# Loading each expert chunk as two half transfers, released and awaited half by half

## The reference, cut to what matters

```python
h = rmsnorm(x, ln_mix);  proj = h @ w_in              # pooling heads and gated DeltaNet heads
x = x + concat([pool_out, dn_out]) @ w_out
h = rmsnorm(x, ln_moe)
top_vals, top_idx = top_k(h @ router_w + router_b, 4) # 4 of 32 experts per token
gates = softmax(top_vals)
for each block of rows of one expert e:
    gt  = minimum(xblk @ w_gate[e] + b_gate[e], 7)
    up  = clip(xblk @ w_up[e] + b_up[e], -7, 7)
    hid = (up + 1) * (gt * sigmoid(1.702 * gt))
    y   = hid @ w_down[e] + b_down[e]                 # added to its tokens times their gates
x = x + y
x = x + (p @ w_ple) * sigmoid(rmsnorm(x, ln_ple) @ w_ple_gate)
return rmsnorm(x, final_norm), and the new pool, conv and delta-rule states
```

## Time and profile before

| | |
|---|---|
| median of the runs | 1196.0 us |
| the profiled execution | 1194.54 us |
| its span, first to last instruction | 1192.8 us |
| PE busy | 1130.2 us, 95% |
| moved by DMA | 435.16 MB, mean 365 GB/s |
| issues of whole expert chunks | 62 gate, 62 up, 57 down in the ring, one gate beside it |

### The profile page before, as it was taken

The page is one execution under the profiler, slowest core; times in us unless marked ns, Lnnn a source line. Parts: engine busy times, 40 slices in busy tenths (PEclk is TensorE's granted clock), DMA queues, the critical chain, the costliest instruction groups (busy, mean ns, idle before and its releaser), DMA issues.

```text
span 1192.8 us, 15407 instructions
## 1 busy us (share of the span) xinstructions
PE 1130.2 (95%) x5906; PEld 485.3 (41%) x5936; DVE 411.5 (34%) x781; ACT 213.7 (18%) x398; POOL 40.0 (3%) x118
## 2 busy tenths in 40 slices
PE   8999999999999999999999898999999999899997
PEld 5667865433333332333333333333333333233333
DVE  5756765843132222132223231323131313131325
ACT  3444232321101021011010101011101101010025
POOL 6002110000000000000000000000000000000000
PEclk9999999999999999999999999999999999999999
DMA  9821539789999999999999999999999999999941
GB/s 315 251 105 71 166 117 333 296 337 424 427 426 428 427 428 428 427 427 429 428 427 429 428 425 428 429 428 427 429 430 428 427 429 429 428 427 427 419 163 45
DMA packets 50603, 435.16 MB, mean 365 GB/s; under 512 B 6861, under 2 KB 14554, under 8 KB 24812
## 3 DMA queue, kind: packets, MB, share of 16 engines
q1 hardware_dynamic: 44425, 430.22, 87.3%
q10 hardware_dynamic: 6123, 4.18, 1.1%
HBM read 429.54 MB, written 4.11 MB: 364 GB/s over the span
## 4 chain that ended last, share of the span: by engine, by line
PE 69%; DMA 21%; DVE 6%; issue 2%; ACT 2%; SPq 0%; POOL 0%; DVEq 0%; ACTq 0%; POOLq 0%
PE ps L1782 40%; DMA ring<-in_w_gate 18%; PE ps L1309 7%; PE ps L1728 4%; PE ps L1619 3%; PE ps L1224 2%; DMA ring<-in_w_up 2%; PE ps L1508 2%; PE ps L1356 1%; PE ps L1749 1%; DVE x_resid L2500 1%; PE ps L1423 1%; PE ps L1996 1%; PE ps L1973 1%; PE ps L1854 1%
## 5 line engine op out<-in xcount | busy, mean ns | idle before, releaser
L1782 PE MATMUL ps<-ring,ht_region 128*64 128x512 f32 (+1 forms) x2152 | 453.7, 599 | 18.9 <-DMA ring<-in_w_gate 18.6
L1782 PEld LDWEIGHTS ps<-ring,ht_region 128*64 128x64 f32 (+1 forms) x2152 | 149.0, 135 | 308.3 <-issue 308.2
L1782 PE MATMUL ps<-ring,q_region 128*64 128x512 f32 (+1 forms) x1088 | 223.6, 594 | 0.3 <-ACT q_region L858 0.3
L1782 PEld LDWEIGHTS ps<-ring,q_region 128*64 128x64 f32 (+1 forms) x1088 | 71.7, 134 | 144.2 <-issue 143.3
L2500 DVE TENSOR_TENSOR x_resid<-ps,x_resid 128x512 f32<-128x512 f32 (+1 forms) x90 | 62.0, 689 | 148.7 <-PE ps L1728 144.5
L2550 DVE SCALAR_TENSOR_TENSOR q_region<-ps,small,u_region 128x1024 f32<-128x1024 f32 x15 | 19.3, 1284 | 222.9 <-ACT u_region L1096 222.9
L1309 PE MATMUL ps<-ht_region,ring 128*128 128x320 f32 x320 | 90.7, 441 | 1.6 <-DVE ht_region L2035 1.0
L2542 DVE TENSOR_SCALAR q_region<-ps 128x1024 f32<-128x1024 f32 x15 | 18.4, 1225 | 165.4 <-PE ps L1782 165.4
L1309 PEld LDWEIGHTS ps<-ht_region,ring 128*128 128x128 f32 x320 | 60.8, 193 | 27.9 <-issue 4.2
L1074 ACT ACTIVATE q_region<-q_region 128x1024 f32<-128x1024 f32 x16 | 16.9, 1056 | 292.3 <-DVE q_region L2524 292.3
L1096 ACT ACTIVATE u_region<-ps,small 128x1024 bf16<-128x1024 f32 x15 | 16.7, 1113 | 226.9 <-PE ps L1782 226.9
(11 more groups left out here) (507 smaller groups left out, 908.6 us busy)
## 6 DMA issues: line engine op xcount, KB each, us to landing
ring<-in_w_gate SPq DMA_DIRECT2D x62, 2048.0 KB, 25.1
ring<-in_w_up SPq DMA_DIRECT2D x62, 2048.0 KB, 22.7
ring<-in_w_down SPq DMA_DIRECT2D x57, 2048.0 KB, 26.8
ring<-in_w_down SPq DMA_DIRECT2D x13, 1024.0 KB, 24.7
ring<-in_w_in SPq DMA_DIRECT2D x4, 2048.0 KB, 16.6
ring<-in_w_out SPq DMA_DIRECT2D x2, 2048.0 KB, 8.9
ring<-in_w_up SPq DMA_DIRECT2D x4, 1024.0 KB, 24.0
ring<-in_w_ple_gate SPq DMA_DIRECT2D x2, 2048.0 KB, 22.3
```

Source lines behind the costliest of these rows:

```text
L1782: ins = mm(PS[s0_:s0_ + width, b0 + hf, :], lhs[:, k, s0_:s0_ + width], rows[:, kk, hf * 512:(hf + 1) * 512], start=False, stop=(k == KT - 1),
```

## The change

All expert chunks are now loaded as two halves of 1 MiB, with one call each. `load_chunk` becomes two calls of `load_half`. `load_two` loads a chunk pair in the order first halves, second halves; before a first half SP waits for `half_used` of the chunk that lay in the slot, before a second half for `used`. `chunk_in[c]` now counts the first half only; the second halves count on `rest_in`, one semaphore per slot (one landing per use; chunk 3 of the first pair, which lies elsewhere, has `home_in`). PE waits for `chunk_in` ahead of row 0 and for the second halves of both chunks ahead of row 2, in every product. The special semaphores of the first and the last pair go away; their halves are issued in the order as before.

```diff
+def rest_count(c):
+
+    return 16 * (c // RING + (0 if c % RING == 3 else 1))
...
+        rest_in = [sem(f"rest_in{c}") for c in range(RING)]
+        home_in = sem("home_in")
...
-        def load_chunk(eng, c, pair_experts, s, home=None):
-
-            cc = c % CPP
-            r = cc % CPM // 2 * RPP * P
-            w = chunk_src["gud"[cc // CPM]][bass.ds(pair_experts[cc % 2], 1)]
-            eng.dma_start(slot(c) if home is None else home,
-                          w[:, r:r + RPP * P, :].rearrange("a (p k) f -> p (a k) f", p=P)).then_inc(s, 16)
...
-        def load_half(eng, c, pair_experts, part, s, home=None):
+        def load_half(eng, c, pair_experts, part, home=None):
...
             eng.dma_start(slot(c)[:, 2 * part:2 * part + 2] if home is None else home,
-                          rows[:, 2 * part:2 * part + 2]).then_inc(s, 16)
+                          rows[:, 2 * part:2 * part + 2]).then_inc(
+                              chunk_in[c] if part == 0 else home_in if c == 3 and home is not None else rest_in[c % RING], 16)
+
+        def load_chunk(eng, c, pair_experts, home=None):
+
+            for part in range(2):
+                load_half(eng, c, pair_experts, part, None if home is None else home[:, 2 * part:2 * part + 2])
+
+        def load_two(eng, c, pair_experts, released, base):
+
+            for part in range(2):
+                for cc in (c, c + 1):
+                    if released:
+                        eng.wait_ge(chunk_used, base + (half_used, used)[part](cc - RING))
+                    load_half(eng, cc, pair_experts, part)
...
                 es = experts_of(turn * 2 + half)
-                for c in range(CPP):
-                    cc = half * CPP + c
-                    sp.wait_ge(chunk_used, turn * (2 * TURN) + used(cc - RING))
-                    load_chunk(sp, cc, es, chunk_in[cc])
+                for c in range(half * CPP, (half + 1) * CPP, 2):
+                    load_two(sp, c, es, True, turn * (2 * TURN))
...
-            for c in range(RING):
-                sp.wait_ge(chunk_used, 2 * MID * TURN + used(c - RING))
+            for c in range(0, CPP, 2):
                 if c < OV_CHUNKS:
-                    sp.wait_ge(ov_used, n_ov * OV_CHUNKS + (c + 1))
+                    sp.wait_ge(ov_used, n_ov * OV_CHUNKS + (c + 2))
                     sp.nop().then_inc(slot_back, 1)
-                load_chunk(sp, c, es, chunk_in[c])
...
+                load_two(sp, c, es, True, 2 * MID * TURN)
...
                                     k = (c - c0) // 2 * RPP + kk
-                                    if kk == 2 and hf == 0 and bias == 2 and half == 0:
-                                        pe.wait_ge(first_half[(c - c0) // 2], 32 if c == c0 else 16)
+                                    if kk == 2 and hf == 0:
+                                        for a_ in range(2):
+                                            cc = half * CPP + c + a_
+                                            if first and cc == 3:
+                                                pe.wait_ge(home_in, 16)
+                                            else:
+                                                pe.wait_ge(rest_in[cc % RING], i * (TURN // RING) * 16 + rest_count(cc))
```

More of the change, by code:

```diff
@@ L362, in trunk_kernel @@
         quarter_used = sem("quarter_used")
-        early_in = sem("early_in")
         wo_used = sem("wo_used")
         quarter_in = sem("quarter_in")
-        up_half = [sem(f"up_half{c}") for c in range(2)]
-        first_half = [sem(f"first_half{c}") for c in range(CPM // 2)]
-        last_half = [sem(f"last_half{c}") for c in range(CPM)]
         chunk_used = sem("chunk_used")
@@ L602, in _ @@
                 if c == 1:
-                    load_half(sp, 1, (0, 1), 1, chunk_in[1])
-                    load_half(sp, RING + 1, (0, 1), 0, chunk_in[RING + 1])
-                else:
-                    cc = RING + 3 if c == 3 else c
-                    load_chunk(sp, cc, (0, 1), chunk_in[cc])
+                    load_half(sp, 1, (0, 1), 1)
+                    load_half(sp, RING + 1, (0, 1), 0)
+                else:
+                    load_chunk(sp, RING + 3 if c == 3 else c, (0, 1))
             is_drained(sp, "kqs0"), is_drained(sp, "kqs1")
@@ L630, in _ @@
             is_drained(sp, "oT2"), is_drained(sp, "oT1")
-            load_chunk(sp, 0, (0, 1), chunk_in[0])
-            load_half(sp, 1, (0, 1), 0, early_in, early_home)
+            load_chunk(sp, 0, (0, 1))
+            load_half(sp, 1, (0, 1), 0, early_home)
             is_filled(sp, "ns3b")
             sp.wait_ge(ssm_stored, 16)
-            load_chunk(sp, 3, (0, 1), chunk_in[3], first_home)
+            load_chunk(sp, 3, (0, 1), first_home)
             sp.wait_ge(wo_used, 1)
-            load_chunk(sp, 6, (0, 1), chunk_in[6])
+            load_chunk(sp, 6, (0, 1))
             sp.wait_ge(s0_stored, 16)
-            load_chunk(sp, 7, (0, 1), chunk_in[7])
+            load_chunk(sp, 7, (0, 1))
             is_filled(sp, "op11a"), is_filled(sp, "op11b")
-            load_chunk(sp, 5, (0, 1), chunk_in[5])
+            load_chunk(sp, 5, (0, 1))
             def experts_of(pair):
@@ L658, in turn_loads @@
                     pair_loads(i + 1, 0)
[L659 to L665, removed]
-                        load_chunk(sp, c, es, chunk_in[c])
[L667 to L676, removed]
+                pair_loads(hi - 1, 1)
             def load_row(c, kk, s):
@@ L689, in _ @@
             sp.wait_ge(chunk_used, used(0))
-            load_half(sp, RING, (0, 1), 1, first_half[0])
+            load_half(sp, RING, (0, 1), 1)
             sp.wait_ge(chunk_used, used(1))
-            load_half(sp, RING + 1, (0, 1), 1, first_half[0])
+            load_half(sp, RING + 1, (0, 1), 1)
             sp.wait_ge(chunk_used, half_used(2))
-            load_half(sp, RING + 2, (0, 1), 0, chunk_in[RING + 2])
+            load_half(sp, RING + 2, (0, 1), 0)
             sp.wait_ge(chunk_used, used(2))
-            load_half(sp, RING + 2, (0, 1), 1, first_half[1])
+            load_half(sp, RING + 2, (0, 1), 1)
             sp.wait_ge(v_mark, VM["table"])
@@ L1763, in product @@
                                     w[1] = first_home
-                                if first and half == 0 and bias == 0 and c == 0:
-                                    pe.wait_ge(early_in, 16)
                                 for kk, hf in (LATE_HALF if final and bias == 2 and c > c0 else IN_ROWS):
                                     k = (c - c0) // 2 * RPP + kk
-                                    if kk == 2 and hf == 0 and bias == 2 and half == 0:
-                                        pe.wait_ge(first_half[(c - c0) // 2], 32 if c == c0 else 16)
+                                    if kk == 2 and hf == 0:
[5 more added lines that the diff above has]
+                                                pe.wait_ge(rest_in[cc % RING], i * (TURN // RING) * 16 + rest_count(cc))
                                     if kk == 2 and hf == 0 and bias == 2 and final and c == c0:
@@ L1772, in product @@
                                         turn_hidden(1)
[L1773 to L1778, removed]
                                     for s0_ in range(0, P, width):
```

## The result

The changed kernel takes 1204.78 us (median of 5 runs, 1204.28 to 1206.38), the kernel before beside it 1195.35 us (5 runs). The ratio is 1.0085, 95% interval 1.007 to 1.010: slower by 9.4 us. The forecast was 1203.2 us and slower, 7.2 us over the runs shown then.

The account below looks back on a forecast made before the run. The full load queue was taken as the bound, with PE's work after its last awaited load. 1194.5 + 11.0 (rate) - 3.5 (start) - 0.3 (waiting by halves) = 1201.7, forecast as median 1203.2 us, range 1198 to 1212.

Parts of the forecast that it names:

- The queue is the bound: Long stage, 300 to 1098 us: transfers never pause; a pair's loads take 58.8 us, PE 55.7, so transfers are slower.
- The rate: Full-queue stretch: halves double a chunk's packets, costing 0.065 us on each of 170 chunks, +11.0 us (8.5 to 18.7).
- that of the rates: Long stage against the tail's halves: 420 instead of 428 GB/s, so 0.09 us more per chunk.
- that of the packet times: Long stage against tail: 617 ns per 16 KB packet, 315 per 8 KB, so 0.11 us more per chunk.
- that of the landings: Late gate chunks against tail halves: landings 4.90 us apart against 4.95 a chunk, so 0.05 us more.
- The start: Where the queue becomes full for good: release by halves sends chunks 16 and 17 out earlier, -3.5 us (0 to -3.5).
- Waiting by halves: PE may begin a gate pair on its first 2 MB: nothing in the middle, -0.3 us at the end.
- The slack of 0.3 us: At the end: last down half lands at 1137.2, PE comes to it at 1137.5, limiting the gain to 0.3 us.
- its rival: At the end, in an experiment's forecast: the last gate wait sets the end, -3.5 us, ratio 0.997; no chance given.
- PE's waits: Twelve more semaphore waits per pair of experts: at most 1.7 us a pair, inside the queue's 3.1; taken as 0.
- The sum: Whole kernel: 1194.5 + 11.0 - 3.5 - 0.3 = 1201.7 us, as median of runs 1203.2 us.
- SP's issues: Load issues per pair go from 12 to 24, 333 ns each, 8 us of 59: hidden.

Follow-up runs that it names:

- e7: Changed kernel, but PE waits ahead of row 0 for both halves of both chunks, except in the first and last pair's products: 1202.64 us, ratio 1.0064 against before.
- e3: Changed kernel, but both halves of a chunk are issued only when the old chunk in the slot is wholly used: 1208.77 us, ratio 1.012 against before.
- e8: Kernel before, with the last pair's gate chunks and first up chunks also loaded as halves, released by whole chunks: 1195.55 us against 1195.11, ratio 1.0003.
- e1: Kernel before with whole 2 MiB chunks, one transfer each, but two 8 KB runs per partition instead of one of 16 KB: 1206.01 us, ratio 1.0103.

## Why the prediction was right, point by point

- **The queue is the bound.** Right. At a full queue the time followed the rate in every kernel with all 128 partitions, and where PE may start (e7) or when loads are released in the middle (e3) changed nothing.
- **The rate.** The mechanism was right and the size too small: 0.065 us a chunk were taken, 0.076 were measured, 12.9 us instead of 11.0. Of the three readings, that of the rates was 0.017 too high, that of the packet times 0.034 too high and that of the landings, at 0.05, 0.026 too low. The low one was misread. I took 26.2 us for the last half, which is the median of two in the earlier trace rows, one of 26.0 and one of 26.3. Asked for alone, the half issued at 1111.0 took 26.3 and landed at 1137.3, and (1137.3 - 1117.4) / 8 = 2.4875 us, 4.975 a chunk, is 0.075 more than 4.90: the size measured, with times rounded to 0.1 us. I leaned to the landings with the reason that a landing releases PE, which says nothing on their precision. That 0.065 still came out near is partly luck, as a choice between one reading that was too low by a slip and two that were too high. The middle slices at 420 to 422 GB/s lie at the slow edge of the 421 to 425 that were named.
- **The start.** Right: -3.5 us forecast, 3.46 us in SP's issue, 3.3 us between the stages of e3 and of the changed kernel.
- **Waiting by halves.** Right in kind: the last down half is what is late next (e8), and in the middle there is nothing (e7). The slack of 0.3 us used the same 26.2 and is 0.1; e8 shows only that it is not the 3.5 of its rival.
- **PE's waits.** Right at 0: the chain of the changed kernel has products of 64 matmuls in 13.88 us, as in the earlier trace rows.
- **The sum.** 12.9 - 3.5 - 0.3 = 9.1, where the stage shows 8.8 and the runs 9.4. The 1.9 us between 7.2 and 9.1 are the rate. With a slack of 0.1 the sum is 9.3.
- **SP's issues.** "333 ns each, 8 us of 59: hidden" had the price wrong and the conclusion right. In the long stage an issue of a half takes 1.9 us in the median, some 45 us of a pair's 60 (here one of three lines of SP's issues, 300 to 1088 us):

```profile
L532 SPq DMA_DIRECT2D ring<-in_w_gate x109: 332/1889/4222, 299.9 to 1079.8; - x109
```

SP stands in the chain of waits with 10% for it, but e1 has half the issues, 0.37 us each in the median, and the same rate. So a row of SP in the chain reads here as waiting for room in the queue, not as SP's work.
- **The rule of the Trainium skill** ("DMA: Bandwidth & Descriptors", Why small descriptors are slow), about 3 cycles a packet and 5.4 us by the estimate: the runs do not agree. The price is 0.076 us for 9 more packets per engine and chunk, 8.4 ns each (9.5 if only the eight data packets count), over twice the 3.5 ns that 3 cycles are by that estimate, and it is paid at 16 and 8 KB already.
- **A sign that failed.** PE's waits for loads should have begun before 600 us. They began after 660 us before and only after 700 in the changed kernel, though its queue is slower. I had counted the queue's rate and not that release and waits by halves let PE run on with less loaded ahead. In the runs: with late release the first wait lies in 620 to 640 us, whether PE waits for whole chunks (e1, apart from two waits of 0.5 us before 500) or by halves (e3); with early release and whole waits (e7) in 640 to 660; with both by halves after 700. The cushion grows and the end does not move, because the queue has no pause to save. The sum of the waits grew as forecast, from 18.8 us (18.6 for gate, 0.2 for up weights) to 24.7 (20.0 and 4.7), with 1.1 for the last down half besides:

```profile
PE ps L1764 <- DMA ring<-in_w_gate: 20.0, 17, 1.4
PE ps L1764 <- DMA ring<-in_w_up: 4.7, 8, 1.3
```

## What to carry to other kernels

Where a load queue is full from some point on, as here, only three things moved the end: when it becomes full, its bytes over its rate, and the work after its last landing; finer release and finer waits in between were worth nothing, however many waits they shortened. A finer split was paid there in packets, by the length of the runs and not by the number or size of the transfers, so try it only at the two ends. And read the price of a smaller piece from a stretch of the trace that already loads such pieces, by bytes over time in the longest stretch there is, and a landing from its own load, not from the median of a group.

## What the runs showed of the hardware that was not expected

- A full queue moved 428 GB/s in runs of 16 KB (2 MiB a transfer), 421 in 8 KB (2 MiB or 1 MiB) and 409 in 4 KB (2 MiB or 512 KB): 9.5 and 9.2 ns for each added data packet of an engine.
- Transfers into partitions 0 to 63 and 64 to 127 in turn moved 218 GB/s at 600 to 700 us, half of 428, and 328 to 344 late in the run, all with the DMA share at 1.00 to 1.01. A full share is not a full rate.
- With the DMA share at 1.01 to 1.03 in all of them, the median issue took 333 ns for whole chunks in runs of 16 KB, 1.9 to 2.0 us for halves in 8 KB, 0.9 to 1.0 us for quarters in 4 KB and 4.7 to 4.8 us for whole chunks in 4 KB. So SP can look busy without being the bound. That the number of packets queued ahead decides it is likely and was not tested by itself.
- The start of the expert stage moved by 3.1 us among these executions, and TensorE's granted clock in the first 30 us was between 0.89 and 1.00 in them; what moves the start is not settled.
